# A feed-forward opening in another order: the first tile without the shift, the first modulation all in row products

## The reference, cut to what matters

```
mod = silu(c) @ ada_w + ada_b               # nine vectors of 1024: sh1, sc1, g1, sh2, ...
h = rmsnorm(x, g) * (1 + sc1) + sh1
x = x + 0.5 * g1 * ((silu(h @ w1) * (h @ w3)) @ w2)     # first feed-forward, D_FF = 2816
...                                         # projection, conv and attention mixer, x += g2 * y
x = x + 0.5 * g3 * swiglu(modulate(rmsnorm(x), sh3, sc3))   # second feed-forward
return rmsnorm(x, final_g)
```

## Time and profile before

| | |
|---|---|
| median of 3 runs | 1038.99 us (1038.23 to 1040.63) |
| the profiled execution | 1040.6 us, its span 1038.9 us |
| busy PE, DVE, ACT, POOL | 97%, 51%, 39%, 6% of the span |
| mean granted clock of PE | 0.988 |
| chain that ended last | PE 92%, of it L757 87% |

### The profile page before, as it was taken

One profiled execution on the slowest core, in us unless ns is written; L12 is line 12 of the kernel. 1 busy time (PEld: TensorE's weight loads), 2 busy tenths in 40 slices (PEclk: granted clock), 3 DMA queues, 4 the chain that ended last, 5 costly groups with the idle time before them and its releaser, 6 DMA issues.

```text
span 1038.9 us, 13277 instructions
## 1 busy us (share of the span) xinstructions
PE 1010.4 (97%) x4539; PEld 822.0 (79%) x4539; DVE 534.8 (51%) x718; ACT 403.0 (39%) x573; POOL 57.7 (6%) x82
## 2 busy tenths in 40 slices
PE   6899999999999999999999999999999999999997
PEld 3478888888888888788877687788888888888886
DVE  2787877768743333634377636643443344433332
ACT  5253443444432222432255533444444344422232
POOL 2111111111000000000000310000000000000000
PEclk9899999999999999999999799999999999999999
DMA  9566876678523333133221112233233332333332
GB/s 336 178 215 202 251 233 210 204 221 262 168 86 112 93 93 96 51 85 98 81 66 41 42 41 62 61 102 101 86 96 101 101 94 88 95 94 97 90 109 81
DMA packets 179000, 127.82 MB, mean 123 GB/s; under 512 B 5424, under 2 KB 166002, under 8 KB 178976
## 3 DMA queue, kind: packets, MB, share of 16 engines
q1 hardware_dynamic: 170544, 97.92, 31.6%
q0 software_dynamic: 8432, 29.58, 8.7%
HBM read 125.39 MB, written 2.10 MB: 123 GB/s over the span
## 4 chain that ended last, share of the span: by engine, by line
PE 92%; DVE 4%; ACT 1%; issue 1%; DMA 0%; POOL 0%; DVEq 0%; ACTq 0%; POOLq 0%
PE pb L757 87%; PE pb L794 1%; PE pb L870 1%; PE pb L776 1%; DVE hl L1232 1%; DVE ubuf L1239 1%; PE pb L801 0%; DMA vec<-in_conv_w_dram 0%; PE pb L1054 0%; DVE acc L1389 0%; DVE probs L1631 0%; PE pb L885 0%; PE pb L1006 0%; DVE hl L1420 0%; PE pb L1034 0%
## 5 line engine op out<-in xcount | busy, mean ns | idle before, releaser
L757 PE MATMUL pb<-hh,wh 128*128 128x512 f32 x912 | 358.8, 393 | 6.5 <-DVE hl L1420 2.3
L757 PE MATMUL pb<-hl,wh 128*128 128x512 f32 x912 | 355.7, 390 | 0.0
L757 PE MATMUL pb<-hh,wl 128*128 128x512 f32 x912 | 355.6, 390 | 0.0
L1200 DVE TENSOR_TENSOR wl<-raw,wh 128x1024 fp32r<-128x1024 f32 x156 | 191.1, 1225 | 273.7 <-ACT wh L413 273.6
L413 ACT ACTIVATE wh<-raw 128x1024 fp32r<-128x1024 f32 x163 | 172.6, 1059 | 404.5 <-PE pb L757 404.5
L757 PEld LDWEIGHTS pb<-hh,wh 128*128 128x128 f32 x912 | 171.6, 188 | 47.9 <-DVE hl L1232 4.6
L757 PEld LDWEIGHTS pb<-hh,wl 128*128 128x128 f32 x912 | 171.6, 188 | 36.0
L757 PEld LDWEIGHTS pb<-hl,wh 128*128 128x128 f32 x912 | 171.7, 188 | 34.5
L757 PE MATMUL pb<-gh,wh 128*128 128x512 f32 x352 | 137.0, 389 | 0.0
L757 PE MATMUL pb<-gh,wl 128*128 128x512 f32 x352 | 136.9, 389 | 0.0
L757 PE MATMUL pb<-gl,wh 128*128 128x512 f32 x352 | 136.9, 389 | 0.0
(11 more groups left out here) (213 smaller groups left out, 724.4 us busy)
## 6 DMA issues: line engine op xcount, KB each, us to landing
raw<-in_ffn_w_dram SPq DMA_DIRECT2D x104, 512.0 KB, 3.9
ada_ring<-in_ada_w_dram POOLq DMA_DIRECT2D x56, 512.0 KB, 5.0
raw<-in_ffn_w_dram SPq DMA_DIRECT2D x32, 448.0 KB, 3.4
raw<-in_w_in_dram SPq DMA_DIRECT2D x17, 512.0 KB, 3.9
ada_start<-in_ada_w_dram SPq DMA_DIRECT2D x16, 512.0 KB, 9.9
raw<-in_w_out_dram SPq DMA_DIRECT2D x8, 512.0 KB, 3.4
x_nat<-in_x_dram SPq DMA_DIRECT2D x4, 512.0 KB, 5.7
out_dram<-o_nat SPq DMA_DIRECT2D x8, 256.0 KB, 2.9
```

Of the source, the lines that this page charges most:

```text
L757: last = pe.matmul(o, a, b, start=start and j == 0 and t == 0, stop=stop and j == len(pairs) - 1 and t == 2)
L1200: dve.tensor_tensor(wl[par][:, :], raw[par][:, :], wh[par][:, :].bitcast(F32), ALU.subtract).then_inc(lo_ready, 1)
```

## The change

- All 32 row products of the opening are done on PE; DVE's chunks and their column sums on PE are gone, with `ADA_ON_PE` and `ADA_ON_DVE`.
- The turns of x come first, then five plain products of 512 columns (`WARM_START`, not used before), then the vectors' turns, which now wait for six and four of the ten small loads apart. Two of x's channel tiles are turned later, behind four row products. DVE copies channels 512 to 1023 of x out of PSUM, ACT the others.
- Tile 0 is multiplied with u, without the shift ("plain": ACT and DVE split u, PE uses banks 5 and 6), between the row products. Its weights have buffers of their own (`wh_first`, `wl_first`; DVE makes the rest part instead of POOL). Then h replaces u in `hh` and `hl` ("shifted"), and tile 1 is multiplied in the opening too, by the same halves of k (`second_steps`, as `plain_steps` but with h, banks 0 and 1).
- The shift's share of tile 0 is made by 32 matmuls of two columns (`bias_steps`; the two columns are the high part and the rest of the shift), summed by DVE to `bias_col`, which enters as the sigmoid's bias and in the two products of SiLU.
- The loop runs over six rounds of three tiles (2 to 19), with tiles 20 and 21 behind it, where the rope angles now lie on DVE. The last modulation vector is multiplied and folded in the first pair of the down product, with PE's L905 product between the first and the second pair.
- POOL starts the ring when the second weight unit of tile 1 has landed. SP loads tile 1's units ahead of two small constant loads.

```diff
-ADA_ON_PE = ((0, 2, 4), (0, 2, 4, 6), (0, 2, 4, 6), (0, 2, 4, 6))
-ADA_ON_DVE = ((1, 3, 5, 6, 7), (1, 3, 5, 7), (1, 3, 5, 7), (1, 3, 5, 7))
-ADA_DONE = (0, 5, 9, 13, 17)
...
-WARM_START, WARM_SQUARES, WARM_ROOT, WARM_NORMED, WARM_HEADS = 7, 11, 4, 14, 9
+WARM_START, WARM_SQUARES, WARM_ROOT, WARM_NORMED, WARM_HEADS = 5, 11, 4, 14, 9
...
-        X_BANK = (0, 1, 2, 3, 4, 5, 6, 0)
+        X_BANK = (0, 1, 2, 3, 4, 5, 0, 1)
+        ROW_BANK = (6, 2, 3, 4)
+        PLAIN_BANK, BIAS_BANK = (5, 6), 2
...
             start_load(0)
+            sp.dma_start(raw[0].rearrange("p (k f) -> p k f", k=DT), w1v[0][:, :, 0:P]).then_inc(raw_landed[0], 16)
             start_load(1)
-            sp.dma_start(raw[0].rearrange("p (k f) -> p k f", k=DT), w1v[0][:, :, 0:P]).then_inc(raw_landed[0], 16)
+            sp.dma_start(raw[1].rearrange("p (k f) -> p k f", k=DT), w3v[0][:, :, 0:P]).then_inc(raw_landed[1], 16)
             start_load(2)
-            sp.dma_start(raw[1].rearrange("p (k f) -> p k f", k=DT), w3v[0][:, :, 0:P]).then_inc(raw_landed[1], 16)
             start_load(3)
+            load(U_A1 + 2, 0, w1v[0][:, :, P:2 * P])
+            load(U_A1 + 3, 1, w3v[0][:, :, P:2 * P])
...
-            for n in range(2):
-                pool.wait_ge(hi_ready, n + 1)
-                pool.tensor_tensor(wl[n][:, :], raw[n][:, :], wh[n][:, :].bitcast(F32), ALU.subtract).then_inc(lo_ready, 1)
...
-            pool.wait_ge(mods_ready, 2)
+            pool.wait_ge(raw_landed[1], 32)
...
             row_copy(0)
+            first_split(0)
+            for k in range(HALF):
+                plain_hi(k)
             row_copy(1)
-            split_hi(0, 0, 16)
+            first_split(1)
+            for k in range(HALF, DT):
+                plain_hi(k)
             row_copy(2)
+            second_split(0)
             act.wait_ge(start_mods, 3)
+            act.wait_ge(plain_used, 1)
             for k in range(HALF):
-                first_hi(k)
-            split_hi(1, 1, 16)
+                shifted_hi(k)
             row_copy(3)
+            second_split(1)
             act.wait_ge(mods_ready, 2)
+            act.activation(shift_pair[:, :, 0:1], mods[:, 0:DT].unsqueeze(2), ACT.Copy).then_inc(shift_ready, 1)
+            act.wait_ge(unit_done, 2)
             for k in range(HALF, DT):
-                first_hi(k)
+                shifted_hi(k)
...
+            act.activation(vcol[:, V_COLS + 9:V_COLS + 10], kst[:, K_COLS:K_COLS + 1], ACT.Sigmoid)
+            act.wait_ge(bias_ready, 1)
+            act.activation(sigb[:, :], pb[PLAIN_BANK[0]][:, :], ACT.Sigmoid, bias=bias_col[:, 0:1]).then_inc(sig_ready, 1)
+            act.wait_ge(g_ready, FREE + 1)
+            act.activation(gh[:, 0, :], gbuf[:, :], ACT.Copy).then_inc(gh_ready, 1)
+            up(U_A1, 0, 1)
...
             pe.wait_ge(ident_landed, 16)
-            pe.wait_ge(x_landed[0], 16)
-            for k in range(DT - 1):
-                turn_x(0, k)
-            pe.wait_ge(vecs_landed, 16 * 10)
...
-            for t in range(1, TT):
+            for t in range(TT):
                 pe.wait_ge(x_landed[t], 16)
-                for k in range(DT - 1):
+                for k in range(DT - 2):
                     last = turn_x(t, k)
                     if t == TT - 1:
                         last.then_inc(x_turned, 1)
-            pe.wait_ge(x_copied, 1)
-            for t in range(TT):
-                last = turn_x(t, DT - 1)
-            last.then_inc(x_turned, 1)
-
-            def start_row(g, k):
+            for _ in range(WARM_START):
+                pe.matmul(pb[6][:, :], ident, x_nat[:, 0, 0:SEQ], start=True, stop=True)
+            pe.wait_ge(vec1_landed, 16 * 6)
...
+            pe.wait_ge(vec2_landed, 16 * 4)
...
+            def start_rows(g, ks):
 
                 v, half = divmod(g, 2)
...
+                for k in ks:
+                    pe.wait_ge(start_landed[g][k // 2], 16)
+                    ins = pe.matmul(pb[ROW_BANK[g]][0:1, :], silu_c[:, k:k + 1],
+                                    ada_start[:, DT * v + k, half * HALF_COLS:(half + 1) * HALF_COLS], start=k == 0, stop=k == DT - 1)
+                    if k == DT - 1:
+                        ins.then_inc(row_done, 1)
 
             def start_sum(g):
 
-                half = g % 2
                 pe.wait_ge(row_copied, g + 1)
                 for col in range(HALF):
-                    pe.matmul(pb[1 + g][:, col:col + 1], ada_rows[0:1, col * P:(col + 1) * P], one_col[0:1, :],
-                              start=col == 0, stop=False, skip_group_check=True)
-                pe.wait_ge(start_step, ADA_DONE[g + 1])
-                for col in range(HALF):
-                    at_ = half * HALF_COLS + col * P
-                    last = pe.matmul(pb[1 + g][:, col:col + 1], acc[:, at_:at_ + P], one_col,
-                                     start=False, stop=True, skip_group_check=True)
+                    last = pe.matmul(pb[ROW_BANK[g]][:, col:col + 1], ada_rows[0:1, col * P:(col + 1) * P], one_col[0:1, :],
+                                     start=col == 0, stop=True, skip_group_check=True)
                 last.then_inc(ada_direct, 1)
+
...
+            def bias_steps(b):
+
+                o = pb[BIAS_BANK][:, 2 * b:2 * b + 2]
+                for k in range(DT):
+                    pe.matmul(o, cols(wh_first[:, b, :], k), shift_pair[:, k, :], start=k == 0, stop=False)
+                    last = pe.matmul(o, cols(wl_first[:, b, :], k), shift_pair[:, k, :], start=False, stop=k == DT - 1)
+                return last
 
             pe.wait_ge(siluc_ready, 1)
             pe.wait_ge(consts_landed, 16)
-            for g in range(3):
-                pe.wait_ge(x_copied, g + 2)
-                for k in ADA_ON_PE[g]:
-                    start_row(g, k)
-                    if g > 0 and k == 0:
-                        start_sum(g - 1)
-                if g == 0:
-                    pe.wait_ge(vec_ready, 3)
-                    norm_spread(N_FFN1)
+            start_rows(0, range(4))
+            turn_last(DT - 2)
+            turn_last(DT - 1)
+            start_rows(0, range(4, DT))
+            pe.wait_ge(vec_ready, 3)
+            norm_spread(N_FFN1)
+            start_sum(0)
+            pe.wait_ge(x_copied, 3)
+            start_rows(1, range(DT))
+            unit(U_A1)
+            pe.wait_ge(x_copied_too, 2)
+            plain_steps(0, (0,))
+            start_sum(1)
+            plain_steps(0, (1, 2, 3))
+            pe.wait_ge(x_copied, 4)
+            start_rows(2, range(4))
+            unit(U_A1 + 1)
+            plain_steps(1, range(HALF)).then_inc(plain_used, 1)
+            start_rows(2, range(4, DT))
+            plain_steps(0, (4, 5, 6))
+            start_sum(2)
+            plain_steps(0, (7,)).then_inc(unit_done, 1)
+            start_rows(3, range(4))
+            plain_steps(1, range(HALF, DT)).then_inc(unit_done, 1)
+            start_rows(3, range(4, DT))
+            unit(U_A1 + 2)
+            second_steps(0, range(HALF))
+            start_sum(3)
+            unit(U_A1 + 3)
+            second_steps(1, range(HALF))
+            pe.wait_ge(shift_ready, 2)
+            bias_steps(0)
+            bias_steps(1).then_inc(bias_done, 1)
+            second_steps(0, range(HALF, DT)).then_inc(unit_done, 1)
+            second_steps(1, range(HALF, DT)).then_inc(unit_done, 1)
 
...
-            pe.wait_ge(x_copied, DT)
-            start_row(3, 0)
-            start_sum(2)
-            unit(U_A1)
-            first_steps(0, range(HALF))
-            for k in ADA_ON_PE[3][1:]:
-                start_row(3, k)
-            unit(U_A1 + 1)
-            first_steps(1, (0, 1))
-            start_sum(3)
-            first_steps(1, (2, 3))
-            first_steps(0, range(HALF, DT)).then_inc(unit_done, 1)
-            first_steps(1, range(HALF, DT)).then_inc(unit_done, 1)
-            with pe.Fori(0, (FT - 1) // 3) as j:
+            with pe.Fori(0, (FT - 4) // 3) as j:
                 for t in range(3):
-                    up_tile(U_A1, 0, 3 * j + t + 1, N_FFN1)
+                    up_tile(U_A1, 0, 3 * j + t + 2, N_FFN1)
                 mod_columns(j + 2)
-            down(U_B1, 0, N_MIX)
+            up_tile(U_A1, 0, FT - 2, N_FFN1)
+            up_tile(U_A1, 0, FT - 1, N_FFN1)
+            down(U_B1, 0, N_MIX, 0, 1)
+            mod_columns(N_MOD - 1)
+            down(U_B1, 0, N_MIX, 1, DT // 2)
...
-            start_chunk(0, 1)
             inverse(N_FFN1)
-            for k in (3, 5, 6, 7):
-                start_chunk(0, k)
-            start_chunk(1, 1)
+            for k in range(HALF, DT):
+                dve.wait_ge(x_turned, k + 1)
+                dve.tensor_copy(xres[:, k, :], pb[X_BANK[k]][:, :]).then_inc(x_copied_too, 1)
             start_mod(0)
-            first_u(0)
-            start_chunk(1, 3)
-            first_u(1)
-            start_chunk(1, 5)
-            first_u(2)
-            start_chunk(1, 7)
-            first_u(3)
-            start_chunk(2, 1)
```

(131 more changed lines are left out.)

118 lines of the change are left out of this document (58 added, 60 removed).

## The result

The kernel after takes 1061.4 us at the median (1059.3 to 1061.7), before 1038.6 (1038.2 to 1040.6): ratio 1.0204, 95% interval 1.0192 to 1.0217. It is slower, as forecast, but by 22.8 us instead of 11.0, and outside the stated range. A second measurement beside other runs gave 1059.5 against 1039.2, 1.0188 (1.0174 to 1.0203).

A forecast was written before the change was run, and what follows sets the result against it. The prediction took PE to bound the kernel, with waits to win only in the opening. Opening +9.6 and fold +1.4 made 11.0 us on 1038.99, so 1050.0 us, range 1045 to 1055.

The forecast's parts named there:

- The row products: Opening on PE: 17 more row products at 0.88 us each cost 15.0 us, with nothing covering them.
- The walk: New opening step by step along PE: first row product 18.6, first plain step 35.7, share from 69.3, end 78.8 us.
- Rival 4: Opening: landing data sets the row products' 0.88 us, half would do without it; kernel faster, 1036 us; chance 0.03.
- The share: Opening, tile 0's shift: 32 two-column matmuls at 0.125 us cost 4.0 us, with 3.2 and 5.6 as ends.
- The 2.4 GHz level throughout: Opening: PE's clock stays at full speed from 20 to 80 us, with no wait for DVE in the walk.
- The hand-over: Ahead of tile 2: PE waits 1.9 us for ACT's and DVE's work; tile 2 starts at 80.7, opening costs +9.6 us.
- The fold: First down pair: the last modulation step and fold end late on DVE, so PE waits 1.4 us.
- The stages from there as long as now: Behind the fold's wait, near 331 us: all later stages keep their length, so nothing is added.
- The sum: Whole kernel: 9.6 for the opening and 1.4 for the fold make 11.0 us more, 1050.0 us.

The follow-up runs named there:

- e6: Kernel before with only the opening's 32 row products all on PE and DVE's chunks with their column products gone: 1049.5 us, ratio 1.0091.
- e3: Kernel after with eight of the share's two-column matmuls behind each of four steps and group 3's column sum two steps earlier: 1059.1 us, ratio 1.0193.
- e5: Kernel after with the two small tiles behind all others, the share's matmuls spread and the last fold one pair later: 1049.6 us, ratio 1.0088.
- e2: Kernel before with only an unused tile of 128 bytes a partition at the place of the two new small tiles: 1046.4 us, ratio 1.0074.
- e14: Kernel after with shift_pair and bias_col behind all other tiles, timed again beside the unedited kernel after on the same chip: 1053.2 us, ratio 1.0117.
- e8: Kernel before with an unused 128-byte tile ahead of hh, moving hh, the weight buffers and gh together: 1039.4 us, ratio 0.9988.
- e4: Kernel after with the last fold's product one pair of the down product later: 1058.5 us, ratio 1.0178.
- e15: Kernel before with five unread filling products in PE's opening waits and one more ahead of group 3's column sum: 1039.8 us, ratio 1.0001.
- e13: Kernel after timed once more, unedited: 1059.5 us, ratio 1.0188.
- e1: Kernel after with shift_pair and bias_col placed behind all other tiles, first timing: 1051.3 us, ratio 1.0109.

## Why the prediction went wrong, point by point

- *The row products: right.* 17 more at 0.88 us, nothing covering them. The walk ran as written: first row product at 18.45 for 18.6, first plain step at 35.55 for 35.7, no wait for DVE. e6 shows the cost alone, 7.0 us in the opening. Rival 4 falls: a product took 0.88 us also at 60.44, with no load landing (DMA share 0.00 from 60 to 66 us).
- *The sizes in the walk: off both ways.* By the start of the share at 70.77 it was 1.5 us behind (69.3 in the walk): each change between row products, sums and steps cost some 0.1 us (1.5 us over some 15 changes), the first tile product behind another kind starting 0.34 instead of 0.23 before its next. The share was 32 x 0.109 = 3.5 us for 4.0, between L784's and L885's price.
- *"The 2.4 GHz level throughout": the step that failed in the opening.* I looked only for idleness as what lowers the clock. It fell behind the share's block of narrow matmuls with PE busy, and the last eight steps took 7.2 us for 5.5, 1.7 us more. e3 and e5 show that it was the block. What that costs at tile 2 is 1.0 to 2.6 us (e3).
- *The hand-over: the wait was 0.2 us for 1.9.* There are two reasons for it: the slow matmuls gave ACT and DVE 1.7 us, and ACT went from the gh copy to its dummy activation without the table load of the earlier trace rows. In the whole first up product the load is gone: the line issues 22 loads for 44, all in the second one, and one new load stands ahead of the loop. Off PE's path that saved nothing elsewhere: a round lasts 32.93 us in both kernels. With the clock up (e3) the wait is 0.6.
- *The fold: right.* PE waited 1.24 us for 1.4.
- *"The stages from there as long as now": the step that failed most.* It says nothing of the two new tiles, which I had read in the diff and priced at nothing without naming them. Through the distance of `gh` from the weights they cost 0.0062 us in each of 1056 matmuls, 6.5 us: e2 alone is 6.4 us over before, and e14 6.3 under after. The sum missed 11.8 us; this is over half of it.
- *The mixer's 2.0 us* are no part of the change that I can name. It took 266.2 us in before and e8, 266.6 in e2, 268.0 in e6 and 268.2 in after. It also took only 266.7 in e4 and e14, which have the change in the opening, and 267.5 in e15, which does not, so it is a difference between executions. The greater part is one group of 42 matmuls, 9.0 to 9.1 us long in some and 10.5 to 10.7 in others, and the granted clock there:

```profile
575.00:580.00 5.00, 4.57 (x30) 1.00 0.00 0
580.00:585.00 5.00, 4.65 (x17) 0.66 0.01 3
585.00:590.00 5.00, 5.00 (x23) 1.00 0.00 0
```

  This is after; in before the same matmuls, 564.73 to 573.71, lie in windows at 1.00. What decides it stays open; it is 1.7 us of the 2.0.
- *What is left.* In spans the parts are 10.6 (opening) + 1.6 (fold: the wait of 1.24 us and the change to its product and back) + 3.1 and 3.5 (pace) + 2.0 (mixer) = 20.8 us, all of it. The medians differ by 22.8 or by 20.3 us, and what that spread is stays open. The warming products are not enough to explain it: they took 4.46 us in some executions (e3, e13, e14) and 5.8 to 6.0 in others (after, e1, e4, e5), but with the share in one block the longer stretch at the low clock took that back, and tile 2 starts at 81.37 in e13 and 81.65 in after.

## What to carry to other kernels

A change that adds a tile moves every tile behind it: look at the distances of PE's moving tiles from its weights before and after, since 128 bytes cost here more than any of the waits that the change was about. Work put on the engine that bounds a stretch must be weighed in full against the waits that it fills: here 17 row products at 0.88 us were 15 us, and with all that went in return the opening was still 7.0 us longer (e6). And a block of narrow matmuls can be followed by the low clock as a wait can.

## What the runs showed of the hardware that I had not expected

- fp32r matmuls of 512 columns start 0.227 us (down) and 0.228 to 0.229 us (up) apart when moving tile and weights lie a multiple of 256 bytes apart in a partition, and 0.233 to 0.234 when they are 64, 128 or 192 bytes off (down 64 and 128, up 128 and 192). Moving both together by 128 bytes changed nothing.
- With PE busy without a gap on 32 two-column matmuls (3.5 us) the granted clock fell to the 1.2 GHz level behind or inside them, for 3.4 us (after) to 6.9 us (e13), in five traces of five; with the same matmuls among wide ones it fell in none of two.
- Two-column matmuls, each with its load of 128 x 128 weights, start 0.11 us apart at the full clock and 0.21 at the low one (e13).
- With a sigmoid placed ahead of the loop the table loads of 1.28 us, one in each tile of it before, were not issued (after, e13). No run places the sigmoid alone.
- A change between kinds of PE work cost about 0.1 us in this opening (1.5 us over some 15 changes, by after's trace).
